# Opening, latent opening, feed-forward seams and dilated first pair of a two-block kernel, changed together

## What is computed

```python
# first block
for i in range(2):
    h = rms_norm(x, pre_norm_g[i])
    y = retention_branch(h) if i == 0 else mla_branch(h)        # 4 heads / 16 latent heads
    x = x + rms_norm(y, post_norm_g[i])
    x = x + (p[i] @ ple_w_proj[i]) * sigmoid(x @ ple_w_gate[i])
# second block
for layer in range(2):
    y = rms_norm(h, mix_norm_g[layer])
    h = h + (chunk_gating_mixer(y) if layer == 0 else dilated_attention_mixer(y))
    y = rms_norm(h, mlp_norm_g[layer])
    h = h + square(relu(y @ w_up[layer])) @ w_down[layer]
return rms_norm(h, final_norm_g)
```

## Time and profile before

| | us |
|---|---|
| median of 3 runs | 2191.73 |
| lowest, highest | 2190.29, 2194.26 |
| profiled execution, its own time | 2194.68 |
| its span (first to last instruction) | 2192.9 |
| TensorE busy | 2138.4 |
| VectorE, ScalarE, GpSimd busy | 1186.1, 890.9, 966.2 |

### The profile page before, as it was taken

How to read it: one execution, slowest core, us unless ns; L and a number is a source line. 1 busy time by engine, 2 the same in 40 slices (tenths; PEclk the granted TensorE clock), 3 DMA queues, 4 the chain that set the end, 5 groups by cost and what they waited for, 6 DMA issues and landing times.

```text
span 2192.9 us, 29461 instructions
## 1 busy us (share of the span) xinstructions
PE 2138.4 (98%) x10254; PEld 1775.5 (81%) x10254; DVE 1186.1 (54%) x1722; ACT 890.9 (41%) x1315; POOL 966.2 (44%) x707
## 2 busy tenths in 40 slices
PE   7999999999999999989999999999999999999996
PEld 6888888778888888868888888887788877888885
DVE  7746556887777776778355222225465556222224
ACT  4423333555555544455533233224334444233223
POOL 4454534355534433316445445444343324445442
PEclk9999999999999999999999999999999999999998
DMA  5232222232222222313222222224221212222221
GB/s 177 73 120 74 93 82 87 88 135 96 77 81 91 77 91 81 125 39 116 96 77 96 96 96 96 96 96 135 77 78 58 78 58 78 96 96 96 96 96 58
DMA packets 37694, 199.96 MB, mean 91 GB/s; under 512 B 4315, under 2 KB 9563, under 8 KB 15228
## 3 DMA queue, kind: packets, MB, share of 16 engines
q1 hardware_dynamic: 28496, 188.76, 24.3%
q10 hardware_dynamic: 9132, 10.31, 1.6%
HBM read 193.81 MB, written 5.24 MB: 91 GB/s over the span
## 4 chain that ended last, share of the span: by engine, by line
PE 88%; DVE 7%; DVEq 2%; ACT 2%; issue 1%; DMA 0%; SPq 0%; ACTq 0%
PE bank L426 15%; PE bank L427 15%; PE bank L432 15%; PE bank L413 12%; PE bank L415 12%; PE bank L414 12%; DVE SS L1647 1%; PE bank L896 1%; PE bank L691 1%; DVE X L1861 1%; PE bank L462 1%; DVE T L1858 1%; DVEq L1646 1%; PE bank L457 1%; PE bank L458 1%
## 5 line engine op out<-in xcount | busy, mean ns | idle before, releaser
L353 POOL TENSOR_TENSOR WL<-RAW,WH 128x512 fp32r<-128x512 f32 x700 | 959.0, 1401 | 1194.4 <-ACT WH L1049 1194.4
L1049 ACT ACTIVATE WH<-RAW 128x2048 fp32r<-128x2048 f32 (+1 forms) x187 | 336.8, 1803 | 593.0 <-PE bank L415 291.0
L426 PE MATMUL bank<-HH,WH 128*128 128x512 f32 x968 | 384.5, 397 | 0.8 <-DVEq L2170 0.8
L427 PE MATMUL bank<-HL,WH 128*128 128x512 f32 x968 | 378.6, 391 | 0.0
L432 PE MATMUL bank<-HH,WL 128*128 128x512 f32 x968 | 241.4, 391 | 0.0
L426 PEld LDWEIGHTS bank<-HH,WH 128*128 128x128 f32 x968 | 182.7, 189 | 40.6 <-issue 1.2
L432 PEld LDWEIGHTS bank<-HH,WL 128*128 128x128 f32 x968 | 181.7, 188 | 40.0 <-issue 2.4
L427 PEld LDWEIGHTS bank<-HL,WH 128*128 128x128 f32 x968 | 182.7, 189 | 38.3 <-issue 1.2
L2136 DVE TENSOR_TENSOR X<-X,bank 128x512 f32<-128x512 f32 x128 | 87.6, 687 | 196.7 <-PE bank L432 117.4
L2127 DVE SCALAR_TENSOR_TENSOR TG<-bank,RS 128x512 f32<-128x512 f32 x64 | 44.0, 688 | 205.1 <-PE bank L415 135.8
L413 PE MATMUL bank<-HH,WH 128*128 128x512 f32 x288 | 112.8, 392 | 5.9 <-DVE HL L1642 5.9
(11 more groups left out here) (421 smaller groups left out, 4385.5 us busy)
## 6 DMA issues: line engine op xcount, KB each, us to landing
RAW<-panels SPq DMA_DIRECT2D x175, 1024.0 KB, 4.8
X<-xin SPq DMA_DIRECT2D x4, 512.0 KB, 9.9
xsave<-X ACTq DMA_DIRECT2D x4, 512.0 KB, 2.8
X<-xsave ACTq DMA_DIRECT2D x1, 2048.0 KB, 12.2
TAB<-scratch ACTq DMA_DIRECT2D x16, 128.0 KB, 2.9
out<-ACC SPq DMA_DIRECT2D x8, 256.0 KB, 2.5
RS<-decay ACTq DMA_DIRECT2D x4, 256.0 KB, 2.6
scratch<-O SPq DMA_DIRECT2D x4, 256.0 KB
```

Of the source, the lines that this page charges most:

```text
L353: gp.tensor_tensor(WL[:, s, cs], RAW[:, s, cs], WH[:, s, cs].bitcast(f32), ALU.subtract).then_inc(lo_ready, 1)
L426: nc.tensor.matmul(o, wh[:, columns[k - k0]], xh[:, k, :], start=first and k == k0, stop=False)
L427: nc.tensor.matmul(o, wh[:, columns[k - k0]], xl[:, k, :], start=False, stop=False)
L1049: return nc.scalar.activation(dst, src, ACT.Copy)
```

## The change

- **Opening.** X is loaded a second time with tokens on the partitions (`xtok`, four tiles of 128 x 1024, into T and U). ScalarE squares these tiles and sums along each row, which gives the token sums directly; squares of the transposed tiles, their adds and the column sums go. Panel 0 is loaded in halves, split by quarters, and its low parts follow by quarters. Constants and positions move to SP's queue. 11 matmuls of ones run in front of the first tile. The bias rows move between the second and the third step of the first tiles. The copy of R moves behind SIN1 and COS1, and panel 3 is split behind it. The value tiles take their banks one by one.
- **Latent opening.** The key tiles use banks 4 and 7; the latent split comes ahead of the turn; key 1 is split ahead of the next panel.
- **Feed-forward seams.** For mlp0 and mlp1 all HH, then all squares; all HL, then all adds.
- **Dilated first pair.** VectorE makes the logits of group 0 behind unit 3's low part.
- `pre0` leaves the list of full norms, with semaphores renumbered; two pairs of semaphores are merged.

```diff
@@ SP
+            half = (slice(0, PANEL // 2), slice(PANEL // 2, PANEL))
             for j in range(4):
                 sp.dma_start(X[:, 2 * j:2 * j + 2, :], xin[2 * j:2 * j + 2].rearrange("k p n -> p k n"))\
                   .then_inc(S[f"x_loaded_{j}"], 16)
-                if j == 0:
-                    load(0, 0)
+                if j < 2:
+                    sp.dma_start(RAW[:, 0, half[j]], panels[0][:, half[j]])\
+                      .then_inc(S["half_loaded"] if j == 0 else raw_loaded[0], 16)
             load(1, 1)
+            sp.dma_start(CONST[:, :], consts).then_inc(S["const_loaded"], 16)
+            sp.dma_start(SIN1[:, :].bitcast(i32), pos).then_inc(S["const_loaded"], 16)
+            for tt in range(NT):
+                sp.dma_start(X_OF_TOKENS[tt], xtok[tt]).then_inc(S["tokens_loaded"], 16)
@@ TensorE
+            pe.wait_ge(S["ones_ready"], 1)
+            for _ in range(11):
+                nc.tensor.matmul(B[7][:, 0:128], ONES[:, :], ONES[:, :], start=True, stop=True)
...
-                    if f == 1 and first:
-                        sum_of_squares("pre0", rows=False, cols=True, banks=(0, 1))
...
                 if first:
                     inverse_rows_of_pre0()
-                    bias_rows()
-                os_ = [bank(tt) for tt in range(NT)]
+                os_ = []
...
+                        if j == 0:
+                            os_.append(bank(tt))
...
-            key_tile(w, 0, 2)
-            key_tile(w, 1, 3)
+            key_tile(w, 0, 4)
+            key_tile(w, 1, 7)
@@ ScalarE
             for k in range(KD):
                 if k == 2:
-                    split_at(0)
+                    split_quarter(0, 0, "quarter_hi_ready")
+                    split_quarter(0, 1, "quarter_hi_ready")
+                if k == 4:
+                    split_quarter(0, 2, "quarter_hi_ready")
+                    split_quarter(0, 3)
                 nc.scalar.activation(HH[:, k, :], x_loaded(k), ACT.Copy, scale=gain("pre0", k)).then_inc(S["norm_hi"], 1)
-                nc.scalar.activation(square_of(k), X[:, k, :], ACT.Square).then_inc(S["norm_sq"], 1)
             split_at(1)
-            root("pre0", D_MODEL, None, True, (0, 1))
-            split_at(2)
-            act.wait_ge(S["pre0_rows"], 1)
-            hi(R[:, :], B[0][:, :]).then_inc(free[0], 1)
             for j in range(2):
                 act.wait_ge(S["bias_rows"], j + 1)
                 hi(ROWS[:, j, :], B[2 + j][0:24, :]).then_inc(free[2 + j], 1)
-            split_at(3)
+            act.wait_ge(S["tokens_loaded"], 64)
+            for tt in range(NT):
+                nc.scalar.activation(X_OF_TOKENS[tt], X_OF_TOKENS[tt], ACT.Square, accum_out=RC[:, 2 * tt:2 * tt + 1])
+            act.drain()
+            nc.scalar.activation(INVERSE_OF_TOKENS, INVERSE_OF_TOKENS, ACT.Sqrt, bias=EPSC[:, 0:1], scale=1.0 / D_MODEL)\
+                .then_inc(S["norm_root"], 1)
+            split_at(2)
             act.wait_ge(S["angle"], 1)
             nc.scalar.activation(SIN1[:, :], ACC[:, 2, :], ACT.Sin).then_inc(S["sines"], 1)
             act.wait_ge(S["angle"], 2)
             nc.scalar.activation(COS1[:, :], ACC[:, 3, :], ACT.Sin, bias=EPSC[:, 2:3], scale=-1.0).then_inc(S["sines"], 1)
+            act.wait_ge(S["pre0_rows"], 1)
+            hi(R[:, :], B[0][:, :]).then_inc(free[0], 1)
+            split_at(3)
...
             split_at(N_MLA + 1)
+            split_h("latent", KC, CKH)
             swapped(T[:, 3, :], T[:, 2, :])
-            split_h("latent", KC, CKH)
...
-            high_qk(0, "k0", 2, MADE_FIRST)
+            high_qk(0, "k0", 4, MADE_FIRST)
+            high_qk(0, "k1", 7, MADE_FIRST)
             split_at(N_MLA + 2)
-            high_qk(0, "k1", 3, MADE_FIRST)
...
                 for k in (2 * j, 2 * j + 1):
-                    gained("mlp0", k, mixed_x(k), N_MLP0 + 1)
+                    high_h("mlp0", k, mixed_x(k), N_MLP0 + 1)
+            for k in range(KD):
+                square("mlp0", k)
             root("mlp0", D_MODEL, RS)
...
-            all_gained("mlp1", updated("x_updated", 2 * KD), N_MLP1 + 1)
+            all_gained_squares_behind("mlp1", updated("x_updated", 2 * KD), N_MLP1 + 1)
@@ VectorE
-            for k in range(1, KD):
-                ve.wait_ge(S["norm_sq"], k + 1)
-                if k > 1:
-                    ve.drain()
-                v.tensor_tensor(SS[:, :], SS[:, :] if k > 1 else square_of(0), square_of(k), ALU.add)\
-                    .then_inc(S["norm_added"], 1)
-            ve.drain().then_inc(S["norm_squares"], 1)
...
                 if f > 0:
-                    gained("mlp0", f - 1)
-            gained("mlp0", KD - 1)
+                    low_h("mlp0", f - 1)
+            low_h("mlp0", KD - 1)
+            for k in range(1, KD):
+                square_added("mlp0", k)
...
                 scaled_unit(n, 2)
-                logits(n, 0)
+                if n > 0:
+                    logits(n, 0)
                 low_qk(n, 2)
                 scaled_unit(n, 3)
                 low_qk(n, 3)
+                if n == 0:
+                    logits(n, 0)
...
                 if f > 0:
-                    gained("mlp1", f - 1)
-            gained("mlp1", KD - 1)
+                    low_h("mlp1", f - 1)
+            low_h("mlp1", KD - 1)
+            for k in range(1, KD):
+                square_added("mlp1", k)
```

More of the change, by code:

```diff
@@ L80 @@
 NORMS = ("pre0", "post0", "pre1", "cq", "ckv", "post1", "mix0", "mlp0", "mix1", "mlp1", "final")
-FULL = tuple(n for n in NORMS if n not in ("cq", "ckv"))
+FULL = tuple(n for n in NORMS if n not in ("pre0", "cq", "ckv"))
 SPLIT = ("pre0", "pre1", "mix0", "mlp0", "mix1", "mlp1")
@@ L244, in program @@
         DEC = RS
-        def square_of(k):
-            return T[:, k, :] if k < 4 else U[:, k - 4, :]
+        X_OF_TOKENS = [t[:, 2 * j:2 * j + 2, :].rearrange("p a n -> p (a n)") for t in (T, U) for j in range(2)]
+        INVERSE_OF_TOKENS = RC[:, :].rearrange("p (t j) -> p t j", j=2)[:, :, 0]
         UNIT_F32 = [R[:, :], SS[:, :], UFS[:, :]]
@@ L349, in _, with low_part @@
         def _(gp):
+            def low_part(s, part):
+                cs = slice(part * PANEL // PARTS, (part + 1) * PANEL // PARTS)
+                gp.tensor_tensor(WL[:, s, cs], RAW[:, s, cs], WH[:, s, cs].bitcast(f32), ALU.subtract).then_inc(lo_ready, 1)
             def low(s):
                 for part in range(PARTS):
[L352 to L357, removed]
+                    low_part(s, part)
+            for part in range(PARTS):
+                if part < PARTS - 1:
+                    gp.wait_ge(S["quarter_hi_ready"], part + 1)
+                else:
+                    gp.wait_ge(hi_ready, 1)
+                low_part(0, part)
+            gp.wait_ge(hi_ready, 2)
+            low(1)
             def both_slots(i):
@@ L447, in tiles_together, with tiles_low_last @@
                 return ends
-            def tiles_low_last(os, w, width, xh, xl, nk, wait):
+            def tiles_low_last(os, w, width, xh, xl, nk, wait, behind_second=None):
                 wh, wl = w[:2]
-                pe.wait_ge(hi_ready, w[2] + 1)
+                if behind_second is None:
+                    pe.wait_ge(hi_ready, w[2] + 1)
                 columns = [[slice(k * width + i * 128, k * width + i * 128 + 128) for i in range(len(os))] for k in range(nk)]
                 for k in range(nk):
+                    if k == 2 and behind_second is not None:
+                        behind_second()
+                    if behind_second is not None and k % 2 == 0:
+                        if k < nk - 2:
+                            pe.wait_ge(S["quarter_hi_ready"], k // 2 + 1)
+                        else:
+                            pe.wait_ge(hi_ready, 1)
                     wait(k)
@@ L500, in head @@
                 w = panel(n, 0)
-                tiles_low_last([bank(4), bank(5)], w, 256, HH, HL, KD, wait_h).then_inc(panel_used, 1)
+                tiles_low_last([bank(4), bank(5)], w, 256, HH, HL, KD, wait_h, bias_rows if first else None).then_inc(panel_used, 1)
                 w = panel(n + 1, 1)
                 for f in range(2):
-                    if f == 1 and first:
-                        sum_of_squares("pre0", rows=False, cols=True, banks=(0, 1))
                     end = tile_of(bank(6 + f)[:, :], w, f, 256, HH, HL, 0, KD)
@@ L1061, in split_quarter @@
                 if part == 0:
-                    act.wait_ge(raw_loaded[slot], m // 2 * 16 + 16)
-                    act.wait_ge(panel_used, m - 1)
+                    if m == 0:
+                        act.wait_ge(S["half_loaded"], 16)
+                    else:
+                        act.wait_ge(raw_loaded[slot], m // 2 * 16 + 16)
+                        act.wait_ge(panel_used, m - 1)
+                if m == 0 and part == 2:
+                    act.wait_ge(raw_loaded[slot], 16)
                 end = hi(WH[:, slot, cs], RAW[:, slot, cs])
```

(14 more changed lines are left out.)

59 lines of the change are left out of this document (35 added, 24 removed).

## The result

The kernel after took 2195.14 us, median of 11 runs (2194.18 to 2196.66). The kernel before took 2191.73, median of 11 runs (2187.04 to 2194.26). The ratio is 1.0017, with a 95% interval of 1.0009 to 1.0024: about 3.4 us slower, less than the 0.2% (4.4 us) that the prediction had set as the least to be told from no change, and still outside the noise. The forecast was 2191.0, on the other side. The size of the difference is loose: in the four sets of runs that were timed with the experiments the same kernel before had medians of 2191.61, 2191.81, 2188.77 and 2192.91.

The account below looks back on a forecast made before the run. TensorE, busy 98% of the span, was taken as the bound, so only its idling or half clock could be won back. Terms summed to -0.8 from 2194.68: 2193.9, less 2.95 gives 2191.0 us; range 2185.0 to 2197.0.

Parts of the forecast that it names:

- the base: Starting point of the sum: the profiled execution of before, 2194.68 us, with 2.95 taken off at the end for the median.
- latent opening: Key tiles on banks 4 and 7: waits on freed banks go, scores start earlier; -1.5 us, between -0.4 and -1.9.
- the clock behind the seams: Slow stretches behind the single waits at mlp0 (1.2) and mlp1 (1.7); +2.9 us, bounds 0 and 6.4.
- the opening: Start of kernel: earlier first matmul lost before bank 0, 0 us; longer slow stretch at the value tiles, +0.8 us.
- the dilated pair: Dilated mixer's first pair: wait for unit 3's low key goes, -2.0 us; slow stretch behind it goes, -3.2, bound 0.
- Rival 2: Opening: GpSimd does not slow the angles, value tiles start at 36.6; 2187.6 or 2186.8 us; chance 0.10.
- longer table switch: Opening, ScalarE: by the skill page about 2.66 us with drain, not 1.28; value tiles 1.4 us later, at 41.4.
- the low part of key 0: Latent opening, VectorE: ready at 549.3 after query 1's at 548.5, so the scores start there, 1.5 us earlier.
- mlp0: First feed-forward seam: TensorE waits for the adds until 1180.6, +2.3 us (0.0 to +5.0); clock +1.2.
- mlp1: Second feed-forward seam: 3.5 us of pieces become one wait of 4.2, -0.1 us (-1.5 to +1); clock +1.7.
- Rival 3: Opening and both seams: every pooled wait ends in a slow stretch costing 3.2 us; 2196.9 us; chance 0.13.
- Rival 1: Seams: ScalarE and VectorE catch up before the sum, so the later squares cost nothing; 2182.4 us; chance 0.10.

Follow-up runs that it names:

- e2: The kernel before with the move of the dilated mixer's first logits alone; 2187.47 us, ratio to before 0.9984.
- e3: The kernel before with the latent opening's banks and order alone; 2188.10 us, ratio to before 0.9992.
- the 35 runs: Timed runs of the kernel before, made beside four of the experiments; in groups from 2187.0 to 2187.4 up to 2194.4 to 2194.7 us.
- e1: The kernel after with the squares and adds of mlp0 and mlp1 put back where they were; 2188.56 us, ratio to before 0.9988.
- e9: The kernel before with the latent and the dilated edit alone; 2186.98 us, ratio to before 0.9992.
- e12: e1 with the swaps of the latent opening ahead of the latent split again; 2189.57 us, ratio to before 0.9986.
- e5: e1 with the copy of R and panel 3's split ahead of the sines on ScalarE; 2182.66 us, ratio to before 0.9953.
- e8: The kernel after with 8 and 17 small matmuls of ones ahead of mlp0's and mlp1's sums of squares; 2191.74 us, ratio to before 0.9997.
- e6: The kernel after with five of seven adds of squares in mlp0 and in mlp1 cut to one column; 2189.97 us, ratio to before 0.9989.
- e7: The kernel after with mlp0's seam put back, leaving mlp1's; 2191.44 us, ratio to before 0.9997.
- e10: The kernel after with mlp1's seam put back, leaving mlp0's; 2191.23 us, ratio to before 1.0008.

## Why the prediction was wrong, step by step

The forecast for the profiled execution was 2193.9 and it took 2196.66, 2.8 more; for the median it was 2191.0 against 2195.14, 4.1 more. The waits came nearly as forecast. What failed is what the clock costs, at two places: behind the seams (+2.9 forecast, 4.3 measured) and in the base together with the dilated stretch. Term by term the 2.8 are: latent opening 0.9, a slow stretch at 963 that was in no term 1.1, the clock behind the seams 1.4, the seams' waits 0.3, less 0.2 at the opening and 0.7 at the dilated pair (5.9 by e2's column).

**The base and the dilated stretch, 1.4 of the 4.1: the failed step.** I summed from a profiled run 2.95 above the median, took 3.2 off for the dilated slow stretch, and then 2.95 to come to the median. e3 and the 35 runs show that the same wait comes with and without that stretch, and that runs as slow as the profiled one are those with the lowest clock, so part of the same gain was taken twice. The dilated edit alone (e2) gained 3.5 to 4.1 and not 5.2: 1.1 to 1.7 too much in the forecast. The run of after lay 1.5 above its median, so 2.95 was 1.4 too much. The right reading would have been a gain of 2.0 for certain, and 3.2 only in those runs that had it to lose.

**The opening: +0.8 forecast, +0.56 measured.** The chain held link by link: the first matmul at 7.51 (about 7 forecast), the rows of pre0 at 33.0 (32), the second half of the angles 28.20 to 37.98 (28.5 to 38.4), the value tiles at 39.28 (40.0). The tokens landed at 21.9 (21.6); the second row, which this reading used, is that of 6 to 16 us. Rival 2 is refuted. The parts were off and cancelled: the value tiles 0.7 early where I had 0, and the slow stretch 1.3 dearer than before's where I had 0.8. TensorE waited 5.2 us and not 7, and the slow stretch was of 6.7. Of the longer table switch that the page "ScalarE: Activation LUTs" of the Trainium skill (What ACT_TABLE_LOAD costs) has, nothing is to be seen: the load that the root needs starts at 26.23 and the root at 27.52, 1.29 later, and the value tiles came 2.1 before the 41.4 that it gave.

**The latent opening: -1.5 forecast, -0.6 measured** (from the first sum to the scores 129.39 before and 128.81 after, 128.64 to 128.96 in e1, e3, e9 and e12). The two waits on freed banks went, as said, and one of 1.28 in front of the scores came in their place. What failed is the low part of key 0 at 549.3. VectorE does the query lows, the rope's and then three low parts in a row:

```profile
547.63 1.39 DVE L1685 TENSOR_TENSOR QR<-TG,QR 64x512 fp32r<-64x512 f32 x2
549.05 2.35 DVE L1685 TENSOR_TENSOR MQL<-bank,MQH 128x512 fp32r<-128x512 f32 x3
```

The low part of query 1 ends at 549.7 and not at 548.5, since the block in front of it does not move (e12). T*SIN, with both inputs in SBUF, took 1.73 us beside GpSimd and 0.68 alone. That agrees with the page "SBUF — State Buffer" of the Trainium skill (Who interferes with whom), by which a VectorE instruction with two inputs in SBUF contends with a GpSimd instruction that reads SBUF. A slow stretch at 963, which took the other 1.1 of this column, was in no term; it is in the profiles of e1, e5 (at 956), e8, e12 and after, and not in those of e6, e7 and e10, whose code is the same there. In after it follows a wait of 1.77.

**mlp0: +2.3 for the wait, 2.27 measured; +1.2 for the clock, 1.7.** The adds ended when forecast, 1181.7 against 1180.6 with 1.0 of that from earlier shifts. The discount on the clock because 2.3 us is near the 1.7 us that did no harm was the wrong choice: it cost what such a stretch costs. Nor is 1.7 us a length that does no harm: the slow stretch near 1784 in before came behind waits of 1.63 and 0.87. The slowest of the 35 adds took 1.62 us in after, so the 1.97 that the forecast worked out from the page "SBUF — State Buffer" of the Trainium skill was not reached here.

**mlp1: -0.1, and 0.1 measured against e2; wait of 4.2 forecast, 4.58 measured; +1.7 for the clock, 2.6: the other failed step.** The pieces turned into one wait, as said, at no cost of their own. All of the seam's loss lies behind it, and 1.7 was the price of the shortest slow stretch, not of one behind a wait of 4.58. In e7 the same wait cost 1.5, so the price varies from run to run. Together with mlp0 the clock was put 1.4 too low.

**The dilated pair: -2.0 and -3.2, measured together -5.8** with a stretch near 1784 that after's run lacks. Right for this pair of runs, and wrong as an expectation (above).

**The rivals.** Rival 3 (a slow stretch of 3.2 behind each of three waits, 2196.9) came nearest: all three stretches came, and cost 2.8 (of which before had some 1.6), 1.7 and 2.6. None was as dear as its 3.2, so that its 2196.9 lies 1.8 above the median. I gave it 0.13 since I took the shortest slow stretch as the measure of all. Rival 1 (the squares catch up) fell on VectorE's and ScalarE's total, as argued.

## What to carry to other kernels

A wait of TensorE of some 2 us or more can cost nearly twice its length, since the matmuls behind it may run at half clock (here 1.77 us was enough once); so pieces of idling had better not be gathered into one, even where their sum stays the same, and where a wait can't be avoided a few matmuls into a bank that is about to be overwritten get the loss behind it back. Before summing from a profiled run, compare its slow stretches with the spread of the timed runs: a stretch that only some runs have can be won only in these. When an operation is moved on a queue that frees a bank, follow the queue to who waits for that bank: here a copy behind two sines ate 7 us that an order change gave back.

## What the runs showed of the hardware

The clock behind a wait is not settled by the wait: 2.01 us of idling, the same code, and a granted clock of 0.54 in the run of before, 1.00 in that of e3. The page "TensorE: Matmul & The Clock Gate" of the Trainium skill (What's actually happening) says that the number of slow matmuls at the start of a kernel varies from run to run with the phase; here this is seen in the middle of a kernel, and in 35 runs that spread over 7.7 us, 0.35%. Small fp32 matmuls of ones (128 columns) held the clock at 1.00 through waits of 2.5 and 4.7 us, with 0.5 and 0.8 us of idling left. In e6 adds of one column still stood 0.52 apart, since four squares of 128x512 on ScalarE took 2.19 us.
